# Gates of the first expert layer: one-hot matrices replaced by indirect adds to a table in DRAM

## The chip, the cores and the metric

The kernel is one program on one core of a Trainium2 chip. The time is the device time of that core in microseconds, as a median over runs; a profile is of one execution of its own. Engines: TensorE (PE; PEld is its weight load), VectorE (DVE), ScalarE (ACT), GpSimd (POOL), SyncE (SP, which here only issues transfers).

## What is computed

Two blocks of two layers each, on 256 tokens of 1024 features in float32. The second block has an attention mixer and then an expert layer in each of its two layers. The expert layer is this, for 16384 experts (128 x 128), 8 heads and 16 picks a head:

```python
q = (xt @ w_q).reshape(T, 8, 2, 128)
s1 = einsum('thd,hnd->thn', q[:, :, 0], sub_keys[0]); s2 = ...      # 128 scores each
v1, i1 = top_k(s1, 16); v2, i2 = top_k(s2, 16)
cand = v1[..., :, None] + v2[..., None, :]                          # 256 sums
best, pos = top_k(cand, 16); expert = (i1 * 128 + i2) at pos
gate = softmax(best)
a = x . w_down[expert]; y = sum(gelu(a) * gate * w_up[expert])
```

## The kernel before

Weights come as a stream of units, each 128 partitions x 1024 float32 (512 KB). SP fetches them into `raw`, a ring of six. For each unit ACT makes the rounded high part `w_hi` (a ring of four, `split`, L509), DVE makes the low part `w_lo` (`split`, L911), and PE multiplies in three passes (high x high, low x high, high x low: L1515, L1516, L1517). ACT and DVE run up to four units ahead of PE; unit n+4 can be split when PE is done with unit n.

The second expert layer gathers the picked rows one by one from a table `both_rows` in DRAM (`gather`, L403, indirect transfers of 128 rows). Its halves are filled earlier by POOL's queue: `relay` in the four feed-forward parts (in L368, out L378) and `copy_up`, 128 transfers of one unit from DRAM to DRAM (L391), of which two are in flight at most: copy n waits for copy n-2.

The first expert layer, where the change is, computes all experts densely and has three stages.

- Down: 128 units. PE computes the features of 128 experts x 256 tokens a unit, ACT puts them through Gelu into `keep[:, c, :]` in `arena` (`activate`, L821) and splits a unit. DVE splits a unit and does one piece of the top-k of one of 16 items (an item is a head and half the tokens; `take` and the pieces `first8` to `decode`). Meanwhile POOL copies: `copy_up(range(COPIES_DOWN))`, 72 units.
- Gates: after the last item DVE, ACT and PE make the softmax and turn the picks so that they stand along tokens. Then, for each group of four tokens, 64 in all, POOL and DVE write `first_hot` (L468, L1458), DVE and ACT write `second_hot` (L1461, L848, L854), PE multiplies them (`gate_matrices`, L1942) into a 128 x 128 matrix of gates a token, and DVE multiplies that into `keep` (`use_gates`, L1470).
- Up: 128 units, each with `chunk_high` (ACT, L879) and `chunk_low` (DVE, L1485) of a chunk of `keep`, and 12 matmuls of PE with 512 columns (four blocks, three passes). POOL first fetches `ln` constants (L485) and then does the other 56 copies.

The order on each engine is the order of the code; waits are on counting semaphores. All transfers of POOL go through one queue, SP's through another.

Of the kernel before, what the change touches and what calls it, by code (L numbers as in the profile page):

```python
# [24 lines left out]
F32 = mybir.dt.float32  # L25
F32R = mybir.dt.float32r
U32 = mybir.dt.uint32
# [4 lines left out]
P = 128  # L32
# [99 lines left out]
COPIES_DOWN = 72  # L132
# [37 lines left out]
def program(nc, stream, x_in_dram, consts, stickc, poolc, scalec, ropec, lnc, subkeys, out):  # L170
    with ExitStack() as ctx:
# [47 lines left out]
        pool_step = sem("pool_step")  # L219
        pool_past = sem("pool_past")  # L220
# [41 lines left out]
        ranks_ready = sem("ranks_ready")  # L262
        hot_ready = sem("hot_ready")
        hot1_done = sem("hot1_done")
        hot2_done = sem("hot2_done")
        hot3_done = sem("hot3_done")
        gates_done = sem("gates_done")
        gates_used = sem("gates_used")
        eh_hi = sem("eh_hi")
        eh_ready = sem("eh_ready")  # L270
# [43 lines left out]
        near = pad[:, 0:HOT * 4 * NK].rearrange("p (s n) -> p s n", n=NK)  # L314
        both_rows = nc.dram_tensor("both_rows", [NK * NK, 2 * D], F32)
# [27 lines left out]
        def _(pool):  # L343
# [74 lines left out]
            for i in range(DEPTH):  # L418
# [18 lines left out]
                norm()  # L437
                x_changed()
            for i in range(DEPTH):
# [3 lines left out]
                if i == 0:  # L443
                    power(0, 16, 4)
                norm()
# [8 lines left out]
                copy_up(range(COPIES_DOWN))  # L454
                pool.wait_ge(hot_ready, t.after(hot_ready, 3))

                first = small[:, 80:80 + 4 * HOT]

                def indices(n):

                    pool.tensor_copy(first, hot[:, 0, bass.ds(n * 4 * HOT, 4 * HOT)]).then_inc(pool_step, 1)
                    pool.wait_ge(pool_step, t.after(pool_step))
                    pool.sem_inc(pool_past, 1)

                def one_hots(s):

                    for j in range(POOL_HOT):
                        ins = pool.tensor_scalar(first_hot[:, s, j, :], iota, first[:, 4 * s + j:4 * s + j + 1],  # L468
                                                 None, ALU.is_equal)
                    ins.then_inc(hot1_done, 1)  # L470

                indices(0)
                for s in range(HOT):
                    one_hots(s)
                with t.loop(T // (4 * HOT) - 1, [(gates_done, HOT), (pool_step, 1), (hot1_done, HOT)]) as n:
                    pool.wait_ge(hot1_done, t.after(hot1_done, HOT))
                    indices(n + 1)
                    for s in range(HOT):
                        pool.wait_ge(gates_done, t.after(gates_done))
                        pool.sem_inc(pool_past, 1)  # L480
                        one_hots(s)
                t.skip(gates_done, HOT)
                t.skip(hot1_done, HOT)
                pool.wait_ge(gates_used, t.after(gates_used, T // 4))
                pool.dma_start(pad[:, :], lnc[2 * i + 1]).then_inc(ln_in, 16)  # L485
                copy_up(range(COPIES_DOWN, NK))
# [5 lines left out]
        def _(act):  # L492
# [141 lines left out]

            def gathered():
# [10 lines left out]

                def exp_gates(n):
                    act.wait_ge(best_ready, t.after(best_ready))
                    e = gates[:, K16 * n:K16 * n + K16]
                    act.activation(e, e, ACT.Exp, bias=stats[:, n:n + 1],  # L650
                                   accum_out=stats[:, 16 + n:17 + n]).then_inc(gates_exp, 1)
# [73 lines left out]
            for i in range(DEPTH):  # L725
# [92 lines left out]
                def activate(c, j):  # L818

                    act.wait_ge(unit_used, t.value(unit_used) + 1)  # L820
                    act.activation(keep[:, bass.ds(c, 1), :].rearrange("p a t -> p (a t)"),  # L821
                                   ps[:, 4 + j % 4, 0:T], ACT.Gelu).then_inc(work_kept, 1)
                    split()

                turn = PAIRS * SPREAD
                with t.loop(NK // turn, [(scores_taken, PAIRS)] + unit_steps(turn)) as n:
                    for j in range(turn):
                        if j == turn - 1:
                            act.wait_ge(scores_taken, t.after(scores_taken, PAIRS))
                        activate(n * turn + j, j)  # L830
                act.wait_ge(scores_taken, t.after(scores_taken))
                for j in range(SPREAD):
                    activate(NK - SPREAD + j, j)
                    if j == SPREAD - 3:
                        act.wait_ge(best_ready, t.after(best_ready))
                        act.activation(pad[:, X_G:X_G + T], pad[:, X_G:X_G + T], ACT.Exp).then_inc(gates_exp, 1)
                act.wait_ge(turned, t.after(turned))
# [22 lines left out]
                for s in range(HOT):  # L860
                    if s + 1 < HOT:
                        distances(s + 1, s + 1)
# [1267 lines left out]
```

## Time and profile before

| | us |
|---|---|
| median of 3 runs (3050.27 to 3056.16) | 3054.75 |
| the profiled execution | 3061.21 |
| its span | 3059.4 |
| PE busy | 2685.5 (88%) |
| DVE busy | 2014.8 (66%) |
| ACT busy | 1320.3 (43%) |
| POOL busy | 859.4 (28%) |

The profiled execution is 6.5 us above the median, so a sum is made against 3061.21 and the difference carried to 3054.75. Shares of the whole say little here, since the program is a row of stages with different limits; the rows further down are by stage.

### The profile page before, as it was taken

The numbers are of one execution on the slowest core, as the hardware profiler recorded it, in microseconds if no ns is written. First come the engines' busy times: TensorE is split into PE (matmuls) and PEld (weight loads), VectorE is DVE, ScalarE is ACT, GpSimd is POOL, SyncE is SP. The second block draws the span as 40 slices with busy tenths as digits, with TensorE's granted clock in tenths as the row PEclk, the third lists the DMA queues.
The fourth block names the chain that finished last, engine by engine and source line by source line (L and its number), as shares of the span: only waits on it lengthen the run. The fifth ranks groups of instructions, "written<-read, shape, count | busy, mean of one in ns | idle before, by whom it ended". The sixth has DMA issues, their size and how long they took to land.

```text
span 3059.4 us, 44794 instructions
## 1 busy us (share of the span) xinstructions
PE 2685.5 (88%) x14826; PEld 2177.4 (71%) x14826; DVE 2014.8 (66%) x3711; ACT 1320.3 (43%) x2261; POOL 859.4 (28%) x1227
## 2 busy tenths in 40 slices
PE   8998799899989989899999679999885687887776
PEld 8987599799879867899999568888775333333322
DVE  6665466666657654477778975555584777777664
ACT  4446544444434444554446744555452222222221
POOL 3432344144325300111001631100001443444442
PEclk9999899999999988999999889999897899999999
DMA  9974299689769942799754039965533999999997
GB/s 344 368 270 138 86 340 366 223 324 369 268 231 365 325 151 91 245 337 345 261 182 151 0 118 340 339 232 192 178 117 127 389 413 412 415 407 408 404 421 304
DMA packets 198902, 841.04 MB, mean 275 GB/s; under 512 B 27552, under 2 KB 27552, under 8 KB 165136
## 3 DMA queue, kind: packets, MB, share of 16 engines
q0 software_dynamic: 99760, 479.01, 40.7%
q1 hardware_dynamic: 99040, 360.75, 33.5%
q8 instruction: 54, 0.88, 0.1%
q14 instruction: 48, 0.39, 0.0%
HBM read 771.49 MB, written 135.27 MB: 296 GB/s over the span
## 4 chain that ended last, share of the span: by engine, by line
PE 53%; DMA 11%; DVE 9%; issue 3%; ACT 3%; POOL 1%; DVEq 0%; ACTq 0%; POOLq 0%; SPq 0%
PE ps L1515 15%; PE ps L1517 15%; PE ps L1516 15%; DMA arena<-both_rows,arena 11%; PE ps L1883 5%; DVE arena L1390 2%; PE ps L1561 1%; PE ps L1663 1%; DVE first_hot L1458 1%; DVE second_hot L1461 1%; DVE w_lo L911 1%; DVE arena L1470 1%; ACT arena L663 1%; ACT w_hi L509 0%; DMA raw<-in_stream 0%
## 5 line engine op out<-in xcount | busy, mean ns | idle before, releaser
L911 DVE TENSOR_TENSOR w_lo<-raw,w_hi 128x1024 fp32r<-128x1024 f32 x681 | 831.2, 1223 | 643.1 <-ACT w_hi L509 637.4
L509 ACT ACTIVATE w_hi<-raw 128x1024 fp32r<-128x1024 f32 x681 | 719.5, 1057 | 675.4 <-PE ps L1517 353.3
L1515 PE MATMUL ps<-act_hi,w_hi 128*128 128x256 f32 x2728 | 779.8, 286 | 20.1 <-DMA arena<-in_subkeys 16.0
L1516 PE MATMUL ps<-act_lo,w_hi 128*128 128x256 f32 x2728 | 773.5, 284 | 0.0
L1517 PE MATMUL ps<-act_hi,w_lo 128*128 128x256 f32 x2728 | 773.3, 283 | 0.0
L1883 PE MATMUL ps<-arena 128*128 128x512 f32 x1024 | 487.8, 625 | 160.1 <-ACT arena L663 160.1
L1515 PEld LDWEIGHTS ps<-act_hi,w_hi 128*128 128x128 f32 x2728 | 524.7, 192 | 29.4 <-DMA arena<-in_subkeys 16.4
L1516 PEld LDWEIGHTS ps<-act_lo,w_hi 128*128 128x128 f32 x2728 | 525.0, 192 | 5.8 <-issue 2.6
L1517 PEld LDWEIGHTS ps<-act_hi,w_lo 128*128 128x128 f32 x2728 | 524.8, 192 | 0.0
L1883 PEld LDWEIGHTS ps<-arena 128*128 128x128 f32 x1024 | 193.6, 197 | 442.5 <-ACT arena L663 235.9
L1390 DVE SCALAR_TENSOR_TENSOR arena<-arena 128x1024 f32<-128x1024 f32 x256 | 313.4, 1224 | 189.0 <-DMA arena<-both_rows,arena 187.7
L403 POOL DMA_INDIRECT arena<-both_rows,arena x256 | 294.5, 1150 | 393.7 <-PE ps L1883 352.0
L378 POOL DMA_DIRECT2D both_rows<-arena x512 | 279.2, 552 | 426.0 <-DVE arena L967 415.9
L1515 PE MATMUL ps<-w_hi,act_hi 128*128 128x512 f32 (+1 forms) x990 | 386.5, 390 | 11.2 <-DVE act_lo L1018 2.8
L1516 PE MATMUL ps<-w_lo,act_hi 128*128 128x512 f32 (+1 forms) x990 | 384.5, 388 | 0.0
L1517 PE MATMUL ps<-w_hi,act_lo 128*128 128x512 f32 (+1 forms) x990 | 384.2, 388 | 0.0
L656 ACT ACTIVATE hot<-hot 128x2 f32<-128x2 f32 x128 | 26.0, 203 | 475.9 <-DVE arena L1390 475.8
L1515 PEld LDWEIGHTS ps<-w_hi,act_hi 128*128 128x128 f32 x990 | 189.1, 191 | 53.1 <-DVE act_lo L939 3.6
L1517 PEld LDWEIGHTS ps<-w_hi,act_lo 128*128 128x128 f32 x990 | 188.9, 191 | 37.9
L1516 PEld LDWEIGHTS ps<-w_lo,act_hi 128*128 128x128 f32 x990 | 189.2, 191 | 37.5
L350 POOL TENSOR_TENSOR small<-small,cst 128x1 f32<-128x1 f32 (+2 forms) x27 | 31.2, 1155 | 647.1 <-DVE small L922 551.3
L391 POOL DMA_DIRECT2D both_rows<-in_stream x128 | 66.2, 517 | 358.0 <-DMA both_rows<-in_stream 354.0
(243 smaller groups left out, 3038.0 us busy)
## 6 DMA issues: line engine op xcount, KB each, us to landing
raw<-in_stream SPq DMA_DIRECT2D x684, 512.0 KB, 5.3
arena<-in_stream POOLq DMA_DIRECT2D x128, 512.0 KB, 8.8
both_rows<-arena POOLq DMA_DIRECT2D x512, 128.0 KB, 6.0
both_rows<-in_stream POOLq DMA_DIRECT2D x128, 512.0 KB, 6.3
pad<-in_ln POOLq DMA_DIRECT2D x4, 1024.0 KB, 6.7
arena<-both_rows,arena POOLq DMA_INDIRECT x256, 10.8
arena<-in_subkeys POOLq DMA_DIRECT2D x2, 1024.0 KB, 5.9
x<-in_x SPq DMA_DIRECT2D x1, 1024.0 KB, 5.0
```

Source lines behind the costliest of these rows:

```text
L350: pool.tensor_tensor(small[:, dst:dst + n], small[:, src:src + n], cst[:, HALF:HALF + 1].broadcast_to([P, n]), ALU.pow).then_inc(rstd_read ...
L378: pool.dma_start(rows.rearrange("(c r) k -> r c k", r=32), arena[32 * a:32 * a + 32, A_RELAY_OUT + UNIT * s:A_RELAY_OUT + UNIT * s + UNIT] ...
L391: pool.dma_start(both_rows[P * n:P * n + P, D:2 * D], stream[UP_1 + n]).then_inc(up_copied[n % 2], 16)
L403: pool.indirect_dma_start(row[:, p % ROW_RING, :], None, both_rows[:, :], at).then_inc(row_in[p % ROW_RING], 16)
L509: act.activation(w_hi[:, u % SPLIT, :], raw[:, u % RAW, :], ACT.Copy).then_inc(hi_done, 1)
L663: act.activation(diags[:, p % DIAG_RING, :], ident, ACT.Copy, scale=weights[:, p:p + 1]).then_inc(diag_ready, 1)
L911: dve.tensor_tensor(w_lo[:, u % RAW, :], raw[:, u % RAW, :], w_hi[:, u % SPLIT, :].bitcast(F32), ALU.subtract).then_inc(lo_done, 1)
L1390: dve.scalar_tensor_tensor(row[:, p % ROW_RING, 0:D], row[:, p % ROW_RING, 0:D], 1.0, x_rows[:, b, :], ALU.mult, ALU.mult, accum_out=dots[ ...
L1515: pe.matmul(dst, lhs[0], rhs[0], start=first, stop=False, **kw)
L1516: pe.matmul(dst, lhs[0], rhs[1], start=False, stop=False, **kw)
L1517: return pe.matmul(dst, lhs[1], rhs[0], start=False, stop=last, **kw)
L1883: ins = pe.matmul(ps[:, 2 * (n % 2) + half, :], diags[:, p % DIAG_RING, :], row[:, p % ROW_RING, D + 512 * half:D + 512 * half + 512], sta ...
```

## The change

The gates stage is taken out. In its place:

- `gate_cells`, a table of 16384 x 256 float32 in DRAM, one cell for each expert and token. It is filled with zeros by 32 transfers of 512 KB (`blank`), 16 at the end of each of the two layers of the first block.
- In the down stage the top-k pieces stand in a plan (`TOPK`: two pieces a unit in the first 8 units, one in each of the next 112), and an eighth piece, `finish_gates`, divides the exponentials of an item. ACT does the exponential of each item (`exp_gates`) at the unit after its `best16`.
- `scatter_gates` on POOL adds the gates: for each item 16 indirect transfers, each with 128 cells of 4 bytes (one a partition) and an add in the transfer. An item waits for its values and for the item two before it to have landed.
- `load_gates` on POOL reads the 128 KB of the table that belong to a unit of the up stage into a ring of four in `hot`. DVE multiplies them in (`weigh_chunk`), two chunks ahead of `chunk_low`.
- The 128 copies are split differently: 16 in the first attention mixer, none in the down stage, 96 between the gate loads of the up stage, 16 in the second mixer (before: 72 in the down stage, 56 in the up stage).

```diff
-COPIES_DOWN = 72
+COPIES_MLA, COPIES_UP = 16, 96
+def topk_plan():
+    pieces = []
+    for n in range(ITEMS):
+        chain = [(j, n) for j in range(7)]
+        pieces += chain[:3] + ([(7, n - 1)] if n else []) + chain[3:]
+    pieces.append((7, ITEMS - 1))
+    plan = [pieces[2 * u:2 * u + 2] for u in range(8)] + [[q] for q in pieces[16:]]
+    return plan + [[]] * (NK - len(plan))
...
+            def blank(part):
+                cells = gate_cells.rearrange("(n p f) o -> n p (f o)", p=P, f=4 * T)
+                half = NK * NK * T // (P * 4 * T) // DEPTH
+                for n in range(half * part, half * part + half):
+                    pool.dma_start(cells[n], hot[:, :, :].rearrange("p n t -> p (n t)")).then_inc(blanked, 16)
+            def scatter_gates():
+                pool.wait_ge(blanked, NK * NK * T // (P * 4 * T) * 16)
+                for n in range(ITEMS):
+                    pool.wait_ge(value_ready, n + 1)
+                    if n >= TB:
+                        pool.wait_ge(scattered[n % TB], 16 * K16 * (n // TB))
+                    for k in range(K16):
+                        q = K16 * n + k
+                        pool.indirect_dma_start(gate_cells[:, :], bass.IndirectOffsetOnAxis(ap=cell[:, q:q + 1], axis=0),
+                                                gates[:, q:q + 1], None,
+                                                compute_op=ALU.add).then_inc(scattered[n % TB], 16)
+            def load_gates(copies):
+                rows = gate_cells.rearrange("(c i t) o -> c i (t o)", c=NK, i=NK)
+                for b in range(TB):
+                    pool.wait_ge(scattered[b], 16 * PICKS // TB)
+                for c in range(NK):
+                    if c >= GATE_RING:
+                        pool.wait_ge(weighted, c - GATE_RING + 1)
+                    pool.dma_start(hot[:, c % GATE_RING, :], rows[c]).then_inc(gates_in[c % GATE_RING], 16)
+                    copy_up(copies[len(copies) * c // NK:len(copies) * (c + 1) // NK])
...
-                copy_up(range(COPIES_DOWN))
-                pool.wait_ge(hot_ready, t.after(hot_ready, 3))
...
+                scatter_gates()
                 pool.dma_start(pad[:, :], lnc[2 * i + 1]).then_inc(ln_in, 16)
-                copy_up(range(COPIES_DOWN, NK))
+                load_gates(range(COPIES_MLA, COPIES_MLA + COPIES_UP))
...
+                def weigh_chunk(c):
+                    dve.wait_ge(work_kept, 2 * H2 + 8 + c + 1)
+                    dve.wait_ge(gates_in[c % GATE_RING], 16 * (c // GATE_RING + 1))
+                    dve.tensor_tensor(keep[:, c, :], keep[:, c, :], hot[:, c % GATE_RING, :],
+                                      ALU.mult).then_inc(weighted, 1)
...
+                for c in range(NK - RING):
                     split()
-                    chunk_low(NK - NK % TURN + RING + j, j % RING)
+                    if c + RING + 2 < NK:
+                        weigh_chunk(c + RING + 2)
+                    chunk_low(c + RING)
```

How POOL's instructions stand around the end of the down stage. Before, after the last of the 72 copies, come the one-hot rows (L468, the last four pairs in a loop) and then, past them, the constants (L485) and the other copies:

```order
470 L391 DMA both_rows<-in_stream 128x1024 [waits up_copied1]
471 L461 COPY small<-hot 128x16 [waits hot_ready]
472 L468 TENSOR_SCALAR first_hot<-cst,small 128x128 [waits pool_step]
473 L468 TENSOR_SCALAR first_hot<-cst,small 128x128 x7
...
489 L468 TENSOR_SCALAR first_hot<-cst,small 128x128
490 L160 REGISTER_ALU
491 L160 COMPARE_AND_BRANCH
492 L485 DMA pad<-in_ln 128x2048 [waits gates_used]
493 L391 DMA both_rows<-in_stream 128x1024 [waits up_copied0]
494 L391 DMA both_rows<-in_stream 128x1024 [waits up_copied1]
```

Of the changed kernel the same place: L419 is `scatter_gates`, L508 the constants, L430 `load_gates`, L438 a copy.

```order
446 L419 DMA gate_cells<-hot 4194304x1 [waits value_ready]
447 L419 DMA gate_cells<-hot 4194304x1 x15
448 L419 DMA gate_cells<-hot 4194304x1 [waits scattered1,value_ready]
449 L419 DMA gate_cells<-hot 4194304x1 x15
450 L508 DMA pad<-in_ln 128x2048
451 L430 DMA hot<-gate_cells 128x256 [waits scattered1,scattered0]
452 L430 DMA hot<-gate_cells 128x256
453 L438 DMA both_rows<-in_stream 128x1024 [waits up_copied0]
454 L430 DMA hot<-gate_cells 128x256
455 L438 DMA both_rows<-in_stream 128x1024 [waits up_copied1]
456 L430 DMA hot<-gate_cells 128x256
457 L438 DMA both_rows<-in_stream 128x1024 [waits up_copied0]
```

So POOL now issues 256 indirect transfers ahead of the first gate load, and afterwards each gate load stands in one queue behind a copy.

How DVE's instructions stand where the up stage begins. Before, the products with the gates (L1470) end, the first six `chunk_low` (L1485) follow, and then a split (L911) and a `chunk_low` a unit:

```order
1016 L1470 TENSOR_TENSOR arena<-ps,arena 128x4x128 [waits gates_done] x4
1017 L1485 TENSOR_TENSOR act_lo<-arena,act_hi 128x256 [waits eh_hi,gates_used]
1018 L1485 TENSOR_TENSOR act_lo<-arena,act_hi 128x256 [waits eh_hi] x5
1019 L160 UNCONDITIONAL_BRANCH
1020 L160 ISA
1021 L911 TENSOR_TENSOR w_lo<-raw,w_hi 128x1024 [waits hi_done]
```

Of the changed kernel: L881 is the split, L1381 `weigh_chunk`, L1386 `chunk_low`.

```order
1309 L881 TENSOR_TENSOR w_lo<-raw,w_hi 128x1024 [waits hi_done] x8
1310 L1381 TENSOR_TENSOR arena<-arena,hot 128x256 [waits gates_in0,work_kept]
1311 L1381 TENSOR_TENSOR arena<-arena,hot 128x256 [waits gates_in1,work_kept]
1312 L1381 TENSOR_TENSOR arena<-arena,hot 128x256 [waits gates_in2,work_kept]
1313 L1386 TENSOR_TENSOR act_lo<-arena,act_hi 128x256 [waits eh_hi]
...
1324 L881 TENSOR_TENSOR w_lo<-raw,w_hi 128x1024 [waits hi_done]
1325 L1381 TENSOR_TENSOR arena<-arena,hot 128x256 [waits gates_in0,work_kept]
1326 L1386 TENSOR_TENSOR act_lo<-arena,act_hi 128x256 [waits eh_hi]
```

The first `chunk_low` now stands behind three products that each wait for a gate load, and in every later unit a gate load is waited for ahead of the `chunk_low` and of the next unit's split.

## Rows read from the trace of the kernel before

**Rows 1.** Windows, busy us (instructions) of each engine: down, gates, up with copies, up without.

```profile
core 0: us, PE busy (x) PEld busy (x) DVE busy (x) ACT busy (x) POOL busy (x), PEclk, DMA share, GB/s
1297.00:1668.00 371.00, 369.73 (x3080) 369.28 (x3079) 281.48 (x693) 183.21 (x268) 30.00 (x58) 1.00 0.77 264
1668.00:1809.00 141.00, 90.52 (x516) 78.81 (x516) 140.35 (x325) 94.55 (x263) 84.53 (x147) 0.85 0.01 3
1809.00:2001.00 192.00, 192.00 (x837) 158.50 (x837) 106.28 (x139) 92.55 (x137) 27.61 (x54) 0.99 0.96 339
2001.00:2158.00 157.00, 157.00 (x694) 130.03 (x693) 89.17 (x112) 78.62 (x113) 0.52 (x1) 1.00 0.61 199
```

**Rows 2.** Timeline: start of the gates stage, start of the up stage.

```profile
1666.33 0.88 PE L1545 MATMUL ps<-cst,pad 128*128 128x128 f32 x6 [0.47 <-ACT arena L821]
...
1807.61 0.61 POOL L485 DMA_DIRECT2D pad<-in_ln  x1 [10.80 <-DVE arena L1470]
...
1809.36 0.80 PE L1515 MATMUL ps<-w_hi,act_hi 128*128 128x512 f32 x1
```

**Rows 3.** DVE's timeline in the down stage: its splits 5 and 119, counted from 0.

```profile
1316.00 1.23 DVE L911 TENSOR_TENSOR w_lo<-raw,w_hi 128x1024 fp32r<-128x1024 f32 x1 [0.31 <-ACT w_hi L509]
...
1645.06 1.23 DVE L911 TENSOR_TENSOR w_lo<-raw,w_hi 128x1024 fp32r<-128x1024 f32 x1
```

**Rows 4.** The page's group of POOL's indirect gather: count, busy us, mean ns.

```profile
L403 POOL DMA_INDIRECT arena<-both_rows,arena x256 | 294.5, 1150 | 393.7 <-PE ps L1883 352.0
```

**Rows 5.** POOL's timeline: two of those issues.

```profile
2366.57 0.94 POOL L403 DMA_INDIRECT arena<-both_rows,arena  x1 [0.30 <-issue]
...
2406.02 1.95 POOL L403 DMA_INDIRECT arena<-both_rows,arena  x1 [0.73 <-PE ps L1883]
```

**Rows 6.** DVE's timeline beside the second of them.

```profile
2405.94 1.22 DVE L1390 SCALAR_TENSOR_TENSOR arena<-arena 128x1024 f32<-128x1024 f32 x1
```

**Rows 7.** Answer on L378, 128 KB a transfer: issue to landing.

```profile
DMA to landing us min/median/max: 3.0/6.0/12.3
```

**Rows 8.** Answer on L403, 1 MB a transfer: issue to landing.

```profile
DMA to landing us min/median/max: 5.5/10.8/16.0
```

**Rows 9.** The page's packets, and one of its lines on transfers (KB, median us).

```profile
DMA packets 198902, 841.04 MB, mean 275 GB/s; under 512 B 27552, under 2 KB 27552, under 8 KB 165136
...
pad<-in_ln POOLq DMA_DIRECT2D x4, 1024.0 KB, 6.7
```

**Rows 10.** Waits from 1809 to 2001: us in total, times, longest.

```profile
POOL both_rows L391 <- DMA both_rows<-in_stream: 157.4, 52, 5.4
...
ACT w_hi L509 <- DMA raw<-in_stream: 72.2, 46, 3.4
```

**Rows 11.** The same from 2001 to 2158.

```profile
ACT w_hi L509 <- DMA raw<-in_stream: 5.0, 4, 2.8
```

**Rows 12.** Windows: first layer's last part, first mixer, second mixer, gather of the second expert layer.

```profile
575.00:616.00 41.00, 34.38 (x158) 28.97 (x158) 19.71 (x26) 19.98 (x26) 1.29 (x4) 0.92 0.42 142
...
1134.00:1233.00 99.00, 86.70 (x398) 67.05 (x398) 46.81 (x95) 44.64 (x89) 0.95 (x1) 0.84 0.27 91
...
2166.00:2320.00 154.00, 137.58 (x657) 113.03 (x655) 110.82 (x204) 81.10 (x132) 1.70 (x4) 0.94 0.44 146
2600.00:2700.00 100.00, 82.94 (x217) 37.81 (x215) 69.29 (x190) 23.52 (x69) 44.84 (x40) 0.95 0.99 404
```

**Rows 13.** POOL's timeline at the norms behind blanks and behind the first mixer's copies.

```profile
613.24 0.55 POOL L350 TENSOR_TENSOR small<-small,cst 128x1 f32<-128x1 f32 x1 [38.11 <-DVE small L922]
...
1233.08 1.46 POOL L350 TENSOR_TENSOR small<-small,cst 128x1 f32<-128x1 f32 x1 [98.13 <-DVE small L922]
```

**Rows 14.** ACT's timeline: the exponential and the table loads around it.

```profile
1661.48 1.28 ACT L836 ACT_TABLE_LOAD   x1
1662.78 0.42 ACT L836 ACTIVATE pad<-pad 128x256 f32<-128x256 f32 x1
```

**Rows 15.** Answer on L391 (copies): issue ns, first and last start.

```profile
L391 POOL DMA_DIRECT2D both_rows<-in_stream x128: 515/515/620, 1250.7 to 2001.6; - x128
```

**Rows 16.** DVE's timeline in the up stage: its product of a chunk.

```profile
1822.28 0.42 DVE L1485 TENSOR_TENSOR act_lo<-arena,act_hi 128x256 fp32r<-128x256 f32 x1
```

More of the change, by code:

```diff
@@ L444, in _ @@
                     power(0, 16, 4)
+                    copy_up(range(COPIES_MLA))
+                else:
+                    copy_up(range(COPIES_MLA + COPIES_UP, NK))
                 norm()
@@ L823, in activate @@
                     split()
[L825 to L836, printed above, removed]
@@ L874, in _ @@
-                t.skip(hot3_done, HOT)
-                t.skip(gates_done, HOT)
-                act.wait_ge(gates_used, t.after(gates_used, T // 4))
-                def chunk_high(c, j):
-                    act.activation(act_hi[:, j, :], keep[:, bass.ds(c, 1), :].rearrange("p a t -> p (a t)"),
-                                   ACT.Copy).then_inc(eh_hi, 1)
-                for j in range(RING):
-                    chunk_high(j, j)
-                with t.loop(NK // TURN, unit_steps(TURN)) as n:
-                    for j in range(TURN):
-                        split()
-                        chunk_high(n * TURN + (RING + j), j % RING)
@@ new lines, in finish_gates @@
+                def finish_gates(n):
+                    dve.wait_ge(gates_exp, t.after(gates_exp))
+                    step(dve.reciprocal(stats[:, 32 + n:33 + n], stats[:, 16 + n:17 + n]))
+                    e = gates[:, K16 * n:K16 * n + K16]
+                    ins = dve.tensor_scalar(e, e, stats[:, 32 + n:33 + n], None, ALU.mult)
+                    if i == 1:
+                        step(ins)
+                    else:
+                        ins.then_inc(value_ready, 1)
+                chain = [first8, first8_at, second8, second8_at, best8, best16, decode, finish_gates]
@@ L1394, in rows_gathered @@
                     split()
-                    for piece in chain:
+                    for piece in chain[:7]:
                         piece(0)
@@ L1417, in _ @@
                     continue
-                dve.wait_ge(work_kept, t.after(work_kept, 2 * H2 + 8))
-                t.skip(work_kept, NK)
-                pieces = [first8, first8_at, second8, second8_at, best8, best16, decode]
-                def pair(n):
-                    take(n)
-                    for j in range(SPREAD):
-                        split()
-                        if j < len(pieces):
-                            pieces[j](n)
-                with t.loop(NK // (PAIRS * SPREAD), [(hi_done, PAIRS * SPREAD), (scores_taken, PAIRS),
-                                                     (dve_step, PAIRS * TOPK_STEPS)]) as n:
-                    for p in range(PAIRS):
-                        pair(n * PAIRS + p)
@@ L1436, in _ @@
-                take(TB * H2 - 1)
-                for j in range(SPREAD // 2):
-                    split()
-                    for piece in pieces[2 * j:2 * j + 2]:
-                        piece(TB * H2 - 1)
-                g3 = pad[:, X_G:X_G + T].rearrange("p (n k) -> p n k", k=K16)
-                step(dve.tensor_copy(small[:, 32:48], g3[:, :, 0]))
-                dve.tensor_tensor(g3, g3, small[:, 32:48].unsqueeze(2).broadcast_to([P, K16, K16]),
-                                  ALU.subtract).then_inc(best_ready, 1)
@@ L1490, in _ @@
-                with t.loop(NK // TURN, [(hi_done, TURN), (eh_hi, TURN)]) as n:
-                    for j in range(TURN):
-                        split()
-                        chunk_low(n * TURN + (RING + j), j % RING)
-                for j in range(NK % TURN - RING):
+                dve.wait_ge(blanked, NK * NK * T // (P * 4 * T) * 16)
+                step(dve.scalar_tensor_tensor(p1[:, 0:P], ident, 1.0, iota, ALU.mult, ALU.mult,
+                                              accum_out=token[:, 0:1]))
@@ new lines, in _ @@
+                step(dve.tensor_scalar(token[:, 1:2], token[:, 0:1], float(P), None, ALU.add))
+                dve.wait_ge(work_kept, 2 * H2 + 8)
+                for u in range(NK):
+                    split()
+                    for piece, n in TOPK[u]:
+                        chain[piece](n)
+                def weigh_chunk(c):
[3 more added lines that the diff above has]
+                                      ALU.mult).then_inc(weighted, 1)
```

254 lines of the change are left out of this document (71 added, 183 removed).

## The prediction

> **What bounds the kernel now.** I read the windows by stage first, then the timeline at the stage's two ends, then the waits. The windows [rows 1] show three kinds of stage. In the down stage PE is busy 369.7 of 371 us: it is the bound, 2.88 us a unit (the splits 5 and 119 of DVE, [rows 3], are 329.1 us and 114 units apart). In the gates stage DVE is busy 140.4 of 141 us, PE has only 90.5, and the transfers stand still (share 0.01). In the up stage PE is busy all the time again. The change goes at the middle stage, and the whole of it lies on the path that sets the end: PE's last down work ends where the turns begin, at 1666.3, and its first up matmul is at 1809.36 [rows 2]. That gap is 143 us, and nothing of it is hidden.
>
> **What takes its place.** A first up matmul needs the chunk of gates it works with, and these need the last add of the table. So I count to the end of POOL's 256 indirect transfers, S, and from there to the first matmul.
>
> *When they start.* The first item's values come from piece 10 of the plan (counted from 0: seven of item 0, three of item 1, then `finish_gates`), two pieces a unit, so in unit 5, whose split was at 1316.0 [rows 3]: with 1.2 us of split and half a microsecond of work, about 1318. The last item's come from unit 119, split at 1645.1: about 1647. The plan keeps 8 units, 23.0 us, between items.
>
> *What one costs on POOL.* The trace of before has no indirect write and no add. The nearest row is the gather, also 128 descriptors by a list of indices: 0.94 us where it is undisturbed, plus 0.30 us to the next [rows 5], so 1.24; by the mean over 256 [rows 4] 1.15 + 0.30 = 1.45. The long ones, up to 1.95 us, lie beside DVE's product of two operands in SBUF [rows 5, 6]. The down stage has such products too (each split is one, 1.23 us of every 2.88), so I take 1.45. The bounds: at 1.24, an item takes 19.8 us, under the 23.0 between items, and the last item decides: S = 1647 + 19.8 = 1667. At 1.45, 16 x 1.45 = 23.2 us an item, POOL is just behind the plan: S = 1318 + 256 x 1.45 = 1689. For an add whose descriptors cost twice the issue, 1.88 + 0.30 = 2.18 us, S would be 1876. I take 1689.
> The Trainium skill, SBUF — State Buffer, section Who interferes with whom, says that a DVE instruction with two SBUF inputs contends with a GpSimd instruction that reads SBUF, and infers that writing the descriptors is not hurt. The rows above bear out the first half. If only the descriptor half counted, the sum would go by 1.24 and end 22 us lower; by the first half it stays.
>
> *From S to the first matmul.* POOL issues the 1 MB of constants (6.7 us, [rows 9]), waits for the last adds to land, and issues the gate loads of 128 KB behind the constants in the same queue. 128 KB land in 3.0 us at best [rows 7]. I take 8 us to the first gates, then three products of DVE of about 0.42 us [rows 16], a high part on ACT and one `chunk_low`: 2.5 us. First up matmul at S + 10.5, so 1699.5 in place of 1809.4: **-110 us**. With the bounds of S, -132 (S 1667) to +77 (S 1876).
>
> **The up stage.** Before, its transfers are the stream (512 KB a unit of 2.73 us: 349 us from 1809 to 2158 for 128 units) and 56 copies. While the copies run, the engines of the queues are busy 0.96 of the time at 339 GB/s, without them 0.61 at 199 [rows 1]. And ACT waits for the stream 46 times, 72.2 us in all, in the first 192 us [rows 10], against 5.0 in the other 157 [rows 11]. PE does not stand still, but this is the edge. Now every unit has the stream (524 KB), 0.75 copies (393 KB) and a gate load (131 KB), together 1.05 MB: 384 GB/s at 2.73 us a unit. At 339 GB/s a unit takes 3.09 us: 128 x 0.36 = +46 us. At the 404 GB/s of the gather [rows 12], whose rows are longer, it costs nothing. Between these I take 350 to 360, near the copies' own row: 2.95 us, 128 x 0.22 = 28, less a few us that the rings of four gate chunks and six units carry: **+25 us**, bounds 0 and +46. DVE's extra product is 0.42 us on 1.57 busy a unit (89.2 us in 157 for 57.5 units, [rows 1]): under 2.73, hidden. POOL's issues, 0.52 us each, are hidden likewise [rows 15].
>
> **The down stage.** PE stays the bound. DVE is busy 281 of 371 us [rows 1], and gets only some 5 small instructions an item more, less a copy of the scores; two pieces a unit in the first 8 units let it fall a few us behind, which the four units of lead hide. ACT gets 16 exponentials with a table load of 1.28 us before and one after [rows 14]: 16 x 2.8 = 45 us on 183 busy of 371, hidden in its waits. The copies leave this stage, and PE had no wait for transfers there: 0.
>
> **Blanks.** 32 transfers of 524 KB, 8.4 MB at the end of either layer. In the window of the first [rows 12] 142 GB/s move for 41 us, 5.8 MB; with 8.4 more it is 346 GB/s, as much as the copies' windows have, where PE is not held up. The issues, 16 x 0.55 = 9 us, lie in the 38.1 us in which POOL waits for the next norm [rows 13]. What spills over delays the stream or the next relay loads: 1.5 us each, **+3 us** (0 to +12).
>
> **Copies moved.** 16 in the first mixer: at the pace of before, 56 copies from 1808 to 2001.6 [rows 15], 3.5 us each, they hold POOL 56 us, of the 98 us that it idles ahead of the norm [rows 13]; the DMA share there is 0.27 [rows 12]. 16 in the second mixer, share 0.44, 154 us long. Both hidden, **+2 us** for a late stream (0 to +8). If the first cover were gone, the norm on POOL would be late by what is over 98 us.
>
> **Sum.** 3061.2 - 110 + 25 + 3 + 2 = 2981 for the profiled execution; 6.5 less against the median: **2975 us**.
>
> **The rivals.**
> *The issue of an add is dear* (ends on the other side). The same chain, but more than 1.45 us a transfer. For: an add needs the cell read and written, and the nearest row is a gather with no add; single issues go up to 1.95 us. Against: the undisturbed issue is 0.94, and descriptors are as many. With the other terms at +30, it decides from (1809.4 - 10.5 - 30 - 1318) / 256 = 1.76 us a transfer; at 2.0 us S is 1830 and the time 3116. Chance 0.17; a price of 1.6 to 1.76, time 3013 to 3055, 0.08.
> *The adds go one after another in memory.* If a transfer of adds is finished only when its cells are read and written, and the next of the queue has to wait for it, each costs the shortest landing, 3.0 us [rows 7], or more: 256 x 3.0 = 768 us, S = 2086, the time 3055 + (2086 + 10.5 - 1809.4) + 30 = 3372; by the gather's shortest landing, 5.5 us [rows 8], it would be 4012. Against: small packets are no burden where the trace has them, 27552 of the 198902 packets are under 512 B [rows 9] beside a gather at 404 GB/s; two items may be in flight. Chance 0.12. The Trainium skill's DMA: Bandwidth & Descriptors, section Specifications, has transfers under 512 B as read-modify-write in any case, and its section Latency and other measured facts a least round trip to memory of about 800 ns. As an estimate by that page, 8 cells an engine at a full round trip each would be 6.4 us a transfer, a worse case than this rival; no row of before shows it.
> *Cheap issues and a wide queue.* 1.24 us and no loss in the up stage: 2975 - 22 - 25 = 2928. For: DVE's products may disturb less here. Against: [rows 10]. It is the lower end of the forecast.
> *The change does nothing*: not possible, the gates stage is gone from the code.
>
> **How the numbers follow.** The forecast's case (1.24 to 1.6 us a transfer, up stage +0 to +46, 2925 to 3014, up to 3035 with the small terms at their ends) has 0.61, dear issues 0.08 and 0.17, serial adds 0.12, and 0.02 for a balance near zero. The range is to leave out no more than 0.2: low 2920, from the cheap case; high 3120, which takes in the first half of the dear issues, 2.0 us a transfer. A difference under 0.2% (6 us) is what a measurement of this kernel cannot tell from none. Faster 0.69, same 0.02, slower 0.29.
>
> **What would show it.** Start to start of the indirect adds on POOL: 1.24 to 1.6 us is right, over 1.76 is the first rival. POOL waiting for the landing of the item two before is the second. The first up matmul within 12 us of the last add. In the up stage: PE's idle time, first of it behind ACT's wait for the stream or DVE's wait for a gate load, and 2.8 to 3.1 us a unit. If a unit is 2.73 us there with the copies at work, the term of +25 was wrong; if POOL's loop of gate loads falls behind and PE idles over 50 us, it was too small.

## The result and the profile after

| | us |
|---|---|
| median of 4 runs (3126.11 to 3134.38) | 3128.96 |
| beside it, the kernel before | 3055.45 |
| ratio | 1.0245 [1.0229, 1.026] |
| the profiled execution, its span | 3134.38, 3132.6 |
| PE busy | 2600.8 (83%) |
| DVE, ACT, POOL busy | 1934.4, 1265.8, 1329.8 |

The change makes the kernel 2.4% slower; 2975 was predicted, at most 3120. PE has 85 us less to do, POOL 470 us more.

The windows by stage, the answer to [rows 1]. The second is the gap between down and up, the last two are the up stage, now with copies all the way.

```profile
core 0: us, PE busy (x) PEld busy (x) DVE busy (x) ACT busy (x) POOL busy (x), PEclk, DMA share, GB/s
1306.00:1677.00 371.00, 369.89 (x3078) 369.23 (x3076) 292.74 (x752) 219.72 (x322) 300.68 (x153) 1.00 0.69 181
1677.00:1870.00 193.00, 0.00 (x0) 0.00 (x0) 0.46 (x1) 0.00 (x0) 161.60 (x105) 0.50 0.23 2
1881.00:2080.00 199.00, 198.24 (x869) 163.70 (x868) 137.61 (x220) 98.59 (x145) 69.83 (x131) 0.99 1.01 384
2080.00:2217.00 137.00, 137.00 (x607) 113.45 (x606) 94.56 (x150) 68.50 (x101) 43.71 (x82) 1.00 1.01 382
```

The down stage is as long as it was. Then for 193 us only POOL works: 104 of the 256 adds start behind PE's last down work, and everything else waits for them. The page's group of the adds and that of DVE's new product say the same:

```profile
L419 POOL DMA_INDIRECT gate_cells<-hot x256 | 461.8, 1804 | 148.0 <-issue 77.7
...
L1381 DVE TENSOR_TENSOR arena<-arena,hot 128x256 f32<-128x256 f32 x128 | 54.1, 423 | 279.1 <-DMA hot<-gate_cells 278.5
```

An add takes 1804 ns on the mean, where I had taken 1150 from the gather [rows 4]; of the 148.0 us that POOL stood idle before adds 70.3 are the one wait for the first values, and 77.7 the 0.30 us between two adds. PE's timeline at the end of down and the start of up, the answer to [rows 2], and POOL's with the last add:

```profile
1674.70 1.19 PE L1475 MATMUL ps<-zero 1*128 1x512 f32 x4
...
1879.02 0.79 PE L1417 MATMUL ps<-w_hi,act_hi 128*128 128x512 f32 x1 [203.13 <-DVE act_lo L1386]
```

```profile
1867.98 1.54 POOL L419 DMA_INDIRECT gate_cells<-hot  x1 [0.30 <-issue]
1868.97 1.19 POOL L508 DMA_DIRECT2D pad<-in_ln  x1
1871.78 1.13 POOL L430 DMA_DIRECT2D hot<-gate_cells  x2 [1.63 <-DMA gate_cells<-hot]
```

From these the difference of the two profiled executions, 3134.38 - 3061.21 = 73.2 us, is put together:

- everything up to PE's last down work: 1674.7 against 1666.3, +8.4;
- the gap: 1879.0 - 1674.7 = 204.3 against 1809.4 - 1666.3 = 143.0, +61.3;
- from the first up matmul to the norm behind the up stage: 354.8 (2233.83 on POOL's timeline) against 353.7 (2163.08), +1.1;
- from that norm to the end: 900.6 against 898.1, +2.4.

Why an add takes so long shows in POOL's and DVE's timelines on both sides of the last split:

```profile
1670.55 2.58 POOL L419 DMA_INDIRECT gate_cells<-hot  x1 [0.30 <-issue]
1673.43 2.57 POOL L419 DMA_INDIRECT gate_cells<-hot  x1 [0.30 <-issue]
1676.31 2.57 POOL L419 DMA_INDIRECT gate_cells<-hot  x1 [0.30 <-issue]
1679.18 1.54 POOL L419 DMA_INDIRECT gate_cells<-hot  x1 [0.31 <-issue]
1681.03 1.55 POOL L419 DMA_INDIRECT gate_cells<-hot  x1 [0.30 <-issue]
```

```profile
1670.48 1.23 DVE L881 TENSOR_TENSOR w_lo<-raw,w_hi 128x1024 fp32r<-128x1024 f32 x1 [1.65 <-ACT w_hi L532]
1673.36 1.22 DVE L881 TENSOR_TENSOR w_lo<-raw,w_hi 128x1024 fp32r<-128x1024 f32 x1 [1.66 <-ACT w_hi L532]
1676.23 1.23 DVE L881 TENSOR_TENSOR w_lo<-raw,w_hi 128x1024 fp32r<-128x1024 f32 x1 [1.65 <-ACT w_hi L532]
```

With DVE still, an add takes 1.54 us, so 1.85 from start to start; the undisturbed gather took 0.94 and 1.24 [rows 5]. And an add that begins just behind a split takes 2.57, 1.03 more. How much more depends on how much of the split is left, as two adds around another split of the down stage show:

```profile
1376.80 1.54 POOL L419 DMA_INDIRECT gate_cells<-hot  x1 [0.30 <-issue]
1378.65 2.13 POOL L419 DMA_INDIRECT gate_cells<-hot  x1 [0.30 <-issue]
...
1378.14 1.23 DVE L881 TENSOR_TENSOR w_lo<-raw,w_hi 128x1024 fp32r<-128x1024 f32 x1 [0.31 <-ACT w_hi L532]
```

The first add begins 1.34 us ahead of the split and isn't longer. The second begins with 0.72 us of the split left and takes 0.58 more. The whole stage goes by this: 152 adds start in it, 87 of them while at least 0.15 us of a split is still to run, and each of the 87 is longer than 1.545 us by what is left of the split less 0.11 to 0.14 us. The 46 that start ahead of a split aren't longer. 43 adds take 2.5 us or more, and all that is lost so is 65 us. From 1330 to 1677 it is 347 us for 153 adds, 2.27 each. The first add began at 1330.0 and the last ended at 1869.5: 2.11 us each over all 256.

### The profile page after: what moved, and what is told of

It reads as the page before. It is cut to its first block, busy times and chain, and to the rows that moved or that the text cites. A ratio compares the mean times of both kernels' runs of the same rounds, so it can differ in the third digit from the quotient of the medians.

```text
span 3132.6 us, 41516 instructions
## 1 busy us (share of the span) xinstructions
PE 2600.8 (83%) x14308; PEld 2101.3 (67%) x14308; DVE 1934.4 (62%) x3582; ACT 1265.8 (40%) x2059; POOL 1329.8 (42%) x1499
## 2 busy tenths in 40 slices
DMA packets 246532, 874.86 MB, mean 279 GB/s; under 512 B 66976, under 2 KB 66976, under 8 KB 212752
## 4 chain that ended last, share of the span: by engine, by line
PE 39%; POOL 16%; DMA 12%; DVE 8%; issue 4%; ACT 3%; POOLq 0%; SPq 0%; DVEq 0%; ACTq 0%
POOL gate_cells L419 15%; PE ps L1417 10%; PE ps L1418 10%; PE ps L1419 10%; DMA arena<-both_rows,arena 10%; PE ps L1785 6%; DVE arena L1339 2%; DMA raw<-in_stream 1%; DVE w_lo L881 1%; PE ps L1565 1%; PE ps L1463 1%; ACT arena L686 0%; ACT w_hi L532 0%; DMA both_rows<-arena 0%; DMA both_rows<-in_stream 0%
## 5 line engine op out<-in xcount | busy, mean ns | idle before, releaser
L881 DVE TENSOR_TENSOR w_lo<-raw,w_hi 128x1024 fp32r<-128x1024 f32 x681 | 831.6, 1224 | 518.0 <-ACT w_hi L532 513.8
L419 POOL DMA_INDIRECT gate_cells<-hot x256 | 461.8, 1804 | 148.0 <-issue 77.7
L1381 DVE TENSOR_TENSOR arena<-arena,hot 128x256 f32<-128x256 f32 x128 | 54.1, 423 | 279.1 <-DMA hot<-gate_cells 278.5
```

The source lines that it names most:

```text
L419: pool.indirect_dma_start(gate_cells[:, :], bass.IndirectOffsetOnAxis(ap=cell[:, q:q + 1], axis=0), gates[:, q:q + 1], None, compute_op=AL ...
L881: dve.tensor_tensor(w_lo[:, u % RAW, :], raw[:, u % RAW, :], w_hi[:, u % SPLIT, :].bitcast(F32), ALU.subtract).then_inc(lo_done, 1)
L1381: dve.tensor_tensor(keep[:, c, :], keep[:, c, :], hot[:, c % GATE_RING, :], ALU.mult).then_inc(weighted, 1)
```

## The experiments

All times are medians of the kernel named; the kernel before ran beside each (3057.1 for the first four, 3057.7 for the next two, 3056.1 for the last), and ratios, with their 95% intervals, are against it.

**1. Writes in place of adds.** Everything else stays; of picks that two heads share, one gate is kept instead of the sum.

```diff
-                                                compute_op=ALU.add).then_inc(scattered[n % TB], 16)
+                                                compute_op=ALU.bypass).then_inc(scattered[n % TB], 16)
```

> The 256 indirect transfers write their cells instead of adding to them (two heads of a token that pick the same expert then keep one gate of the two). Theory A (the add makes the issue dear: 1.54 us where undisturbed, against 0.94 for the gather's list of indices): the issue falls to about 0.94 us undisturbed, a mean near 1.15, start to start about 1.45, the last transfer near 1705 instead of 1868, time about 2970. Theory B (it is the indirect write, or the 4-byte cells, that make it dear, whatever is done with them): issue stays 1.54 undisturbed and 1.80 mean, time 3129. Theory C (the issue waits for the memory behind it): the landing of a transfer shortens and the issue with it, some value between.

Measured: 3056.6 us, ratio 0.9986 [0.9958, 1.0015]; its eight runs lie from 3027.59 to 3066.18, further apart than those of any other kernel here. The answers on POOL's line, first of the changed kernel, then of this one (count, shortest, middle and longest issue in ns, first and last start):

```profile
engine op xcount: duration ns min/median/max, first and last start us, forms
L419 POOL DMA_INDIRECT gate_cells<-hot x256: 1541/1548/2582, 1330.0 to 1868.0; - x128
```

```profile
L419 POOL DMA_INDIRECT gate_cells<-hot x256: 962/968/2013, 1328.2 to 1779.8; - x128
```

A write costs 0.97 us, all but the gather's 0.94. So the scatter is not what is dear, nor the cells' addresses: it is the add, 0.58 us a transfer. What makes the add dear inside POOL stays open. It isn't the number of data packets: a gather of 128 rows is 128 of them and a write 16, at nearly the same price. But the time did not fall to theory A's 2970, since another thing appeared: the down stage itself became longer, and ended at 1784.5 in place of 1674.7, though POOL now waited 160.6 us for values (70.3 of them for the first, as in the changed kernel). The first up matmul came at 1793.1. The waits in that stage ("issue" is time in which an engine waited for nothing that the profile shows), and two windows of 10 us in it:

```profile
POOL gate_cells L419 <- DVE hot L1316: 160.6, 14, 70.3
...
PE ps L1419 <- issue: 18.5, 32, 2.0
PE ps L1418 <- issue: 15.3, 26, 1.5
PE ps L1417 <- issue: 13.6, 31, 1.0
```

```profile
1360.00:1370.00 10.00, 3.89 (x13) 3.23 (x12) 1.62 (x3) 1.33 (x2) 7.57 (x8) 0.50 0.18 53
1380.00:1390.00 10.00, 10.00 (x86) 10.00 (x85) 6.66 (x19) 5.25 (x8) 5.58 (x5) 1.00 0.50 170
```

PE starts 13 matmuls in the first window and 86 in the second. The queues are not full (share 0.18). The granted clock is 0.50 in the first window, the lower of its two levels, after PE has begun to pause (in the window ahead of it it is 0.83), so the matmuls that do start are longer too (0.41 us and more for 0.28): only about half of the 110 us are waits. Every wait of PE of over 0.25 us in that stage belongs to a burst of writes: POOL has then written for at least 10 us without a pause (here since 1328), and the last one ends no later than 2.6 us behind the burst; three of the bursts of 16, which take 22 to 24 us each, have no such wait. Experiment 6 takes this up.

**2. Half the adds.** Picks 0, 2, 4 and so on alone; the gates of the others are left out.

```diff
-                    for k in range(K16):
...
+                    for k in range(0, K16, 2):
```

> Only every second pick of an item is added to the table (8 transfers an item instead of 16; the other gates stay zero), everything else the same. Theory A (POOL's issues are the whole of the loss): 128 x 2.1 = 269 us from 1330 end before the down stage does, the last item's 8 end some 20 us after its values are ready, so the first up matmul comes about 10 us after the last down one instead of 204: time 3129 - 190 = 2939. Theory B (something else holds the up stage back too, for instance the landing of the adds, 3.3 us each, if they queue): the gap stays over 30 us with fewer issues, time 2960 or more.

Measured: 2940.98 us, 0.9612 [0.959, 0.9635]. PE's first up matmul:

```profile
1685.56 0.79 PE L1418 MATMUL ps<-w_hi,act_hi 128*128 128x512 f32 x1 [12.15 <-DVE act_lo L1387]
```

POOL now waits for values between items, and PE's wait is down to 12 us, against 203. Gate loads, copies and blanks are unchanged, and behind the first up matmul the profiled execution is as long as that of the changed kernel (1255.3 and 1255.4 us). So the 191 us that the wait fell by went with the adds alone. Theory A has it.

**3. DVE's split in four pieces.** In the down stage the product of 1024 columns becomes four of 256.

```diff
-                    dve.tensor_tensor(w_lo[:, u % RAW, :], raw[:, u % RAW, :],
-                                      w_hi[:, u % SPLIT, :].bitcast(F32), ALU.subtract).then_inc(lo_done, 1)
+                    step_at = UNIT // parts
+                    for lo in range(0, UNIT, step_at):
+                        ins = dve.tensor_tensor(w_lo[:, u % RAW, lo:lo + step_at], raw[:, u % RAW, lo:lo + step_at],
+                                                w_hi[:, u % SPLIT, lo:lo + step_at].bitcast(F32), ALU.subtract)
+                    ins.then_inc(lo_done, 1)
...
-                    split()
+                    split(1, 4)
```

> In the down stage DVE makes the low part of a unit in four products of 256 columns instead of one of 1024; same work. In the trace an add that runs beside this product of 1.23 us takes 2.57 us instead of 1.54. Theory A (an add's issue is shut out for the whole of one DVE instruction with two operands in SBUF): with pieces of 0.3 to 0.4 us it is held for a piece, or gets in between them; the long issues fall from 2.57 to about 1.9 and the mean in the down stage from 1.97 to about 1.7, POOL issues some 20 more adds by the end of that stage, time 3129 - 35 = 3094. Theory B (the issue needs a time free of DVE's reads, and pieces back to back give none): long issues stay near 2.6, time 3129.

Measured: 3074.48 us, 1.0056 [1.0034, 1.0078]. POOL's timeline at the place of the fence above, DVE's beside it, and PE's first up matmul:

```profile
1669.20 1.54 POOL L419 DMA_INDIRECT gate_cells<-hot  x1 [0.30 <-issue]
1671.05 1.75 POOL L419 DMA_INDIRECT gate_cells<-hot  x1 [0.30 <-issue]
1673.10 1.54 POOL L419 DMA_INDIRECT gate_cells<-hot  x1 [0.30 <-issue]
...
1670.62 1.43 DVE L883 TENSOR_TENSOR w_lo<-raw,w_hi 128x256 fp32r<-128x256 f32 x4 [1.44 <-ACT w_hi L532]
...
1825.77 0.79 PE L1420 MATMUL ps<-w_hi,act_hi 128*128 128x512 f32 x1 [149.74 <-DVE act_lo L1389]
```

DVE does the same work, in 1.43 us for 1.23, and the add beside it takes 1.75 in place of 2.57. The mean add falls from 1804 to 1592 ns; 256 x 0.212 = 54.3 us; the last add ended 54.0 us earlier in the profiles, and the medians differ by 54.5. So an add is not slowed in proportion: it is shut out until the DVE instruction that got there first is over, and short instructions let it in. The Trainium skill, SBUF — State Buffer, section Who interferes with whom, says that a DVE instruction with two SBUF inputs contends with GpSimd's reads, and that the second to issue blocks until the first is done. These rows agree (1.03 us lost behind a product of 1.23, 0.21 behind pieces of 0.3 to 0.4). Of its inference that writing descriptors is not hurt, they say only that the indirect transfer as a whole is; no run separates its reads from its descriptors.

**4. The blanks elsewhere.** All 32 go to the first mixer, and its 16 copies to the second.

```diff
-COPIES_MLA, COPIES_UP = 16, 96
+COPIES_MLA, COPIES_UP = 0, 96
...
-                if i == 0:
-                    pool.wait_ge(blank_ready, 1)
-                blank(i)
...
-                    copy_up(range(COPIES_MLA))
+                    pool.wait_ge(blank_ready, 1)
+                    blank(0)
+                    blank(1)
```

> All 32 blank transfers stand in the first attention mixer of the second block, where the 16 copies stood; the 16 copies are made in the second mixer (32 there). Theory A (each of the two bursts of 8.4 MB made the stream late behind it and cost 4.3 us): both costs go, the start of the down stage comes at 1297 to 1299 instead of 1305.9; 16 more copies in the second mixer cost up to 5 us more there: time 3121 to 3127. Theory B (16.8 MB in one burst do the same or worse to the mixer's own stream): the start of the down stage stays at 1305 or later, time 3129 to 3140.

Measured: 3127.91 us, 1.0226 [1.0207, 1.0246], so 1 us of the 8.4 came back, which lies between its two theories. POOL's norm behind the mixer, in the changed kernel and in this one ([rows 13] has 1233.08):

```profile
1242.12 1.47 POOL L367 TENSOR_TENSOR small<-small,cst 128x1 f32<-128x1 f32 x1 [53.32 <-DVE small L892]
```

```profile
1240.70 1.46 POOL L367 TENSOR_TENSOR small<-small,cst 128x1 f32<-128x1 f32 x1 [89.17 <-DVE small L891]
```

The cost moved with them: from `ropec`'s transfer to this norm it is 132.3 us (1108.40 to 1240.70) where it was 125.0. The cover of the mixer isn't better than that of the layers' ends, at least not for all 32 in one burst; the place and the length of a burst changed together here.

**5. Half by adds, half by one-hots.** At 2.11 us some 160 adds fit between the first, at 1330.0, and the end of down, at 1674.7; there are 256. Items are half the tokens each, so I gave the first 128 tokens to the table, now 8 MB, with 16 blanks and loads of 64 KB, and the second 128 to the one-hot matrices of the kernel before. An item waits for the one before it to land.

```diff
-                for n in range(ITEMS):
+                for n in range(H2):
                     pool.wait_ge(value_ready, n + 1)
-                    if n >= TB:
-                        pool.wait_ge(scattered[n % TB], 16 * K16 * (n // TB))
+                    if n:
+                        pool.wait_ge(scattered[0], 16 * K16 * n)
...
+                with t.loop(P // (4 * HOT) - 1, [(gates_done, HOT)]) as n:
+                    for s in range(HOT):
+                        use_gates(n * HOT + s, s)
+                        one_hots(n * HOT + (HOT + s), s)
```

> A version made from what the runs have shown. The 128 transfers of the first 128 tokens (8 items, each waits until the one before has landed) are added to a table of 8 MB, with 16 blanks and gate loads of 64 KB; the second 128 tokens take their gates from the one-hot matrices of the kernel before, 32 groups in place of 64. Theory A (POOL's cost of an add is what decided): 8 items x (16 x 2.27 + 3.7) = 320 us from 1325, done at about 1645, before PE's last down work at about 1671. The gap then holds only the one-hot groups, 32 x 2.1 = 67 us fewer than 143: first up matmul at about 1671 + 76 = 1747. With half the blanks (+4.5), up stage +1 and copies +2.5 on the profiled 3061: about 3002. Rival B (the gap does not scale with the groups, since DVE's weighing of the whole chunk set and the gate loads come on top): 3020 to 3035. Rival C (an item's landing takes much longer under the down stage's traffic than the 3.3 us seen after it, 10 us or more): POOL ends after 1700, the gap grows by the rest, 3030 to 3060.

Measured: **2989.37 us**, 0.9777 [0.976, 0.9793]: faster than both, by 2.2% and 4.5%. Theory A had 3002. POOL's last adds, PE's last down work and its first up matmul:

```profile
1644.80 1.55 POOL L428 DMA_INDIRECT gate_cells<-hot  x1 [0.30 <-issue]
1648.58 1.20 POOL L437 DMA_DIRECT2D hot<-gate_cells  x2 [2.24 <-DMA gate_cells<-hot]
...
1665.95 0.28 PE L1534 MATMUL ps<-act_hi,w_lo 128*128 128x256 f32 x1
...
1739.72 0.79 PE L1532 MATMUL ps<-w_hi,act_hi 128*128 128x512 f32 x1 [0.19 <-DVE act_lo L1501]
```

The adds are done 20 us before the down stage is, and the gap is 73 us, against 143: 32 groups fewer at 2.1. That is theory A's mechanism, with 12 us less than its sum. The 12 us have their place too: with 8 blanks a layer in place of 16 the two norms of [rows 13] are at 613.72 and 1233.59, half a microsecond late each, so half the blanks cost 0.5 us at most and not 4.5; the gap took 2.5 less; the up stage took 353.3 us (to the norm at 2092.99) and what follows 896.4, together 2 us under the kernel before, where I had 3.5 over it.

**6. Half the writes.** The edits of experiments 1 and 2 together; every second pick's gate is left out.

> As e1 (plain writes instead of adds), but with every second pick alone, so bursts of 8 transfers in place of 16; the other half of the picks' gates is left out. In e1 PE stood in the down stage with nothing to wait for, always in the second half of a burst of writes. Theory D (the stall comes only once many writes are queued behind one another): with bursts of 8 there is none, the down stage takes 371 us as in the kernel before, first up matmul about 1690, time 2940 to 2945. Theory E (each write costs PE the same, 95 us over 256): half of it, about 47 us, down stage 418 us, time about 2990.

Measured: 2935.29 us, 0.96 [0.9581, 0.9619], from two runs. PE's waits in the down stage:

```profile
PE ps L1420 <- issue: 0.7, 2, 0.4
PE ps L1418 <- issue: 0.3, 1, 0.3
PE ps L1419 <- issue: 0.3, 1, 0.3
```

1.3 us in place of 47.4. Bursts of 8 writes, some 10 us long, don't hold PE up; most bursts of 16 do. Theory D's numbers came, theory E's did not. But the burst got shorter and the pause behind it longer in one edit, so whether the length of a burst or the rate of writes decides is not shown, and neither is what keeps PE from starting matmuls.

**7. Adds of 64 cells.** All 256 transfers, with partitions 0 to 63 alone; the gates of the other tokens are left out.

```diff
-                        pool.indirect_dma_start(gate_cells[:, :], bass.IndirectOffsetOnAxis(ap=cell[:, q:q + 1], axis=0),
-                                                gates[:, q:q + 1], None,
+                        pool.indirect_dma_start(gate_cells[:, :], bass.IndirectOffsetOnAxis(ap=cell[0:64, q:q + 1], axis=0),
+                                                gates[0:64, q:q + 1], None,
```

> As the changed kernel, but each of the 256 adds takes the picks of partitions 0 to 63 alone, 64 cells in place of 128; the gates of the other half of the tokens are left out (of each block the second 64). Alone, after the down stage, an add of 128 cells took 1.54 us, a write 0.97. Theory F (what an add costs more than a write is paid for each cell): about 0.8 to 1.0 us; POOL's adds then cost 1.1 to 1.3 us with the gap, POOL waits for the values, the last add is at about 1650, first up matmul at about 1690, time about 2943. Theory G (a fixed price for each transfer): 1.4 to 1.54 us as before, still held beside DVE's split; last add 1840 to 1868, time 3105 to 3128.

Measured: 3067.32 us, 1.0042 [1.0023, 1.0062]. The answer on POOL's line:

```profile
L419 POOL DMA_INDIRECT gate_cells<-hot x256: 1397/1402/2442, 1332.8 to 1809.8; - x128
```

1.40 us for 64 cells, 1.54 for 128. A line through these two, an estimate, is 2.2 ns a cell on about 1.26 us a transfer. Theory G holds for the issue: most of the price is one for each transfer. Half the cells save 0.14 us of it; to save the rest takes fewer transfers. The time came out below its range, 3105 to 3128: from start to start it is 1.87 us on the mean (1332.8 to 1809.8) against 2.11, 0.24 less, of which 0.14 is the add itself; the rest lies beside DVE.

## Why the prediction was wrong

**The price of an add failed.** The step is *What one costs on POOL*: "so I take 1.45", S = 1689. The adds took 2.11 each and S was 1869.5, 181 us later. Of this, 12 us are the start (1330.0 for 1318: down began 9 us later, and the first values took 3 more), 256 x 0.66 = 169 the price. I had it from an undisturbed gather of 1.24 and 0.21 for DVE's disturbance. The base is 1.85 (experiment 1: it is the add's; 0.58 us more than a write). The disturbance is 0.42 in the down stage and 0.26 over all 256. So of the 0.66 the base is 0.61 and the disturbance 0.05. The base alone lies over the 1.76 from which the prediction had the change lose. The case that came is the first rival, *the issue of an add is dear*, with 0.17. Its sum at 2.0 us was 3116; at 2.11 it would be 28 us more, 3144, where 3129 came, since it carried +30 for small terms that came to 12.

The bound above, 2.18, held the price. What was wrong was to place the price at the gather's for no better reason than that both have 128 descriptors. The gather's rows could tell the price of addressing, and did: the write costs the same. They had nothing on what the add does. With a bound at 1.24 and one at 2.18, and the profit gone at 1.76, 0.25 for all above 1.6 was too little.

**DVE's disturbance** was seen in the right rows ([rows 5, 6]) and undersized, 0.21 for 0.42 in the down stage. Those rows give the rule that the adds then kept: the gather begins 0.08 us into a product of 1.22 and takes 1.01 more. But I took its weight as a mean from the gather stage. In the down stage POOL issues without a pause, and 87 of 152 adds begin while a split runs. It is the smaller part of the miss; experiment 3 got 54 of its 65 us back.

**From S to the first matmul**: 10.5 predicted, 9.5 from the end of the last add (1869.5 to 1879.0). Right.

**The up stage** was predicted at +25 and came to +1.1. The windows have 384 GB/s with PE busy 198.2 of 199 us. I had taken the copies' own row, 339 GB/s at a share of 0.96 [rows 1], for a limit. It was none, whatever the share said. In that stage POOL waited for each copy two before ([rows 10], 157.4 us), so the pace may have been that of two copies in flight and not of the queues; no run changed the number in flight, and this is not shown. The waits from 1881 to 2080 show the new edge:

```profile
POOL both_rows L438 <- DMA both_rows<-in_stream: 125.8, 55, 4.0
ACT w_hi L532 <- DMA raw<-in_stream: 91.0, 68, 3.2
DVE arena L1381 <- DMA hot<-gate_cells: 50.1, 41, 3.6
...
PE ps L1417 <- DVE w_lo L881: 0.8, 1, 0.8
```

ACT waits for the stream, DVE for gates, and PE for 0.8 us: the rings carry it. The gather stage's 404 GB/s [rows 12] was a better guide than 339.

**The blanks** cost 8.4 us, not 3, inside their range of 12. Each of the two bursts of 16 cost 4.2: between POOL's norms ahead of and behind the first (576.11 and 618.93) are 42.8 us, for 38.7 in the kernel before. Experiment 4 shows that they cost it in the mixer too. In experiment 5, with bursts of 8, the same stretch is 38.7 again: half of them cost nothing there, and its 0.5 us are late already at the norm ahead of the first blanks. **The copies moved** were put at 2. In the first mixer they cost nothing: between the norms of [rows 13] are 619.8 us in the kernel before and 619.9 in experiment 5, with its 16 copies. The 2.4 us behind the up stage may not be theirs either, since experiment 5 has the same copies there and is 1.7 us shorter than the kernel before; that is as fine as single executions tell. **The down stage** stayed PE's, as said, and no engine got near it. Two small readings were off, and nothing hangs on them: DVE's busy time a unit in the up stage is 1.55 us (89.2 for 57.5), not 1.57, and an exponential with its two table loads is 2.98 us by [rows 14], not 2.8.

**Serial adds** didn't come: POOL never waited for the landing of the item two before. One argument that I held against them was no argument, though. The 27552 packets under 512 B [rows 9] are no small pieces of data: they are 4 bytes each, 16 for every one of 1722 transfers, and only 4048 of them fall behind 2400 us, where the gather is. The trace of before had nothing on transfers of single cells. The 6.4 us a transfer that the prediction estimated from the Trainium skill's DMA: Bandwidth & Descriptors, section Latency and other measured facts, did not come either: undisturbed adds follow each other at 1.85 us with the queues' engines at a share of 0.23.

## What to carry to other kernels

An operation that the trace does not have is not priced by its nearest neighbour: where 256 of it lie on the path, multiply both bounds by the count first, see which side of zero they end on, and give the far one its chance. Small indirect transfers are paid by the transfer far more than by the cell; count them against the time of the engine that issues them, and give that path only as many as fit beside other work. Half of a change may be worth more than all of it: where one resource is free for a while and then binds, fill it to that point and leave the rest to the old way. And where DVE has time left and works beside POOL while that issues such transfers, cut DVE's long products of two SBUF operands into pieces: it cost 0.2 us of DVE a unit here and gave back 54 us of POOL.

## What the runs showed of the hardware

- An indirect add of 128 cells holds POOL 1.54 us, an indirect write 0.97, an indirect gather 0.94; an add of 64 cells 1.40. All have 0.30 us to the next.
- DVE's product of 1.23 us with two operands in SBUF lengthens an add that begins during it, by what is left of the product less 0.11 to 0.14 us (87 of 87), up to 2.57 us in all. An add that begins ahead of the product is not longer (46 of 46). Beside four pieces of the same work it is 1.75.
- The add's cells travel one by one: packets under 512 B are 66976 with adds and 38304 with writes, 28672 = 256 x 112 fewer, so a write of 128 cells is 16 packets (of 32 bytes) and an add 128 (of 4). Alone, the adds of 193 us (one every 1.85 us) held the queues' engines to a share of 0.23, which was no limit here.
- Most bursts of 16 writes at 1.27 us keep PE from starting matmuls for a time (47.4 us of waits "issue", granted clock down to 0.50, a down stage 110 us longer); bursts of 8 don't, and adds, which are slower, don't either. The cause is open.
- Bursts of 16 transfers of 512 KB at the end of a layer delayed it by 4.2 us each, bursts of 8 not at all.
- A stream, copies and gate loads together ran at 384 GB/s with PE busy 198.2 of 199 us.
